# The forgetting bias of the attention logits as one bf16 product of three parts

## Chip, core and metric

One core of a Trainium2 chip runs the whole program in one launch. The metric is the device time of that core in microseconds (us), as the median of several runs; smaller is better.

## What is computed

The reference is one layer of an encoder: 16 learned tokens are put ahead of 512 frames of width 1024; a mixer made of forgetting attention and a state-space scan (S5) adds to the residual, then a product-key expert layer (PEER) adds to it, then a norm. All arrays are float32. What the change touches is the bias of the attention logits:

```python
log_f = jax.nn.log_sigmoid((f + b_forget).astype(jnp.float32))
cum = jnp.cumsum(log_f, axis=1)
s = jnp.einsum('bqhd,bkhd->bhqk', qb, kf)
s = s + cb[..., :, None] - cum_k[:, :, None, :]
s = jnp.where(mask, s, NEG_INF)
p = jax.nn.softmax(s, axis=-1)
```

The term of the query (`cb`) is constant along a softmax row and drops out, so the kernel adds only the negative running sum over the keys.

## The kernel before

The 512 frames are worked in two halves of 256 (hf = 0, 1), each of two tiles of 128 queries. For each half the program runs projections (queries, keys, values, the scan's input u), then a **mixer pass**, then branch products, the output product, a second norm and the query lists of the expert layer. The 512 gathered expert rows per partition (L635 on POOL, L1294 and L1297 on VectorE) are spread over what follows: 12 before the second pass, two with each of its steps, and so on by fixed counts, the rest in the last loop, which streams the expert tables through TensorE (L920, L929) from about 860 us to the end.

Each engine has its own instruction list, written out by hand, and they meet through semaphores; a table `order` at the top gives each product its pair of PSUM banks. A mixer pass has 16 steps. Step i handles one (tile j, head h) of the attention and one block i of 128 states of the scan, side by side:

- TensorE: `logits` of step i+1; a quarter of a gate product (`gate_part`, L681); the scan's output product `c_times_x` (L724, L725), which waits for POOL's `state`; another quarter; the transposes of the probabilities (L747, L749); a quarter; probabilities times values (L759, L761); a quarter; the scan's input products `b_times_u` (L715) for the step after.
- VectorE: the row maximum of the logits (L1356), then the scan's recurrence `recur` (L1182, L1324 to L1329), then the normalisation of the probabilities (L1360, L1361), in the second pass two expert rows (L1294).
- POOL: `state` (L579 to L586), in the second pass two gathers (L635).
- ScalarE: exponentials (L1004) and evacuations.

Tile j sees 16 + 128 (j+1) keys, so the four blocks of eight heads have 144, 272, 400 and 528 keys (blocks 0 and 1 in the first pass, 2 and 3 in the second). `logits` makes three kinds of products into one pair of banks: queries times keys (L737, 64 rows deep), the bias (L739), and the causal mask (L740, bf16, 128 columns). With 528 keys L737 and L739 are two products each of 264 columns. The bias is a product of a stationary operand that is one column of the identity, repeated 128 times (8 rows deep), and the 8 x 528 array `ncum`, the negative running sums of the eight heads. Both are float32; a float32 product stands in the profile as two MATMUL rows and two LDWEIGHTS rows, a bf16 product as one of each.

`ncum` is made once, on 8 partitions, before the first pass: VectorE adds the bias and forms a log-sigmoid with ScalarE (L1269 to L1275), clears an addend (L1276) and scans (L1277); the scan signals `ncum_ready`, for which TensorE waits before its first pass. Meanwhile POOL builds the table of rotations for the scan (L544 to L555, after L1080 gives sine and cosine) and signals `table_ready` behind L558, for which VectorE waits before its first pass. POOL's constants (identity, mask and others, L513 to L523) are made at the very start and signal `consts_ready`.

Of the kernel before, what the change touches and what calls it, by code (L numbers as in the profile page):

```python
# [15 lines left out]
ALU = mybir.AluOpType  # L16
# [3 lines left out]
BF16 = mybir.dt.bfloat16  # L20
# [3 lines left out]
P = 128  # L24
# [4 lines left out]
L = META + SEQ  # L29
TT = SEQ // P  # L30
HEADS = 8
# [41 lines left out]
O_ATT = O_VM + AW  # L73
# [9 lines left out]
O_NCUM = O_KEYS + HK * NKEY  # L83
# [29 lines left out]
def hybrid_program(nc, x, meta, g_mix, g_ffn, g_ffn_row, g_out, w_u, w_k, w_q, w_v, w_f, w_g, b_f, b_g, w_att, w_val,  # L113
# [53 lines left out]
    with ExitStack() as ctx:  # L167
        sb = lambda name, shape, dt=F32: ctx.enter_context(nc.sbuf_tensor(name, shape, dt))
        sem = lambda name: ctx.enter_context(nc.semaphore(name))
        gate_all = sb("gate_all", [P, G_WORDS])  # L170
# [14 lines left out]
        ident = sb("ident", [P, P])  # L185
        identb = sb("identb", [P, P], BF16)
        maskb = sb("maskb", [P, P], BF16)

        gathered = ring[:, 0:SLOTS, :]  # L190
# [25 lines left out]
        def shaped(v, shape):  # L216
            if len(shape) == 1:
                return v
            if len(shape) == 2:
                return v.rearrange("p (a b) -> p a b", a=shape[0])  # L220
            if len(shape) == 3:
                return v.rearrange("p (a b c) -> p a b c", a=shape[0], b=shape[1])
            return v.rearrange("p (a b c d) -> p a b c d", a=shape[0], b=shape[1], c=shape[2])

        def region(off, *shape):
            return shaped(gate_all[:, off:off + math.prod(shape)], shape)
# [8 lines left out]
        small, carry = region(O_SMALL, 34, NT), region(O_CARRY, 8, NT)  # L235
        gates, merged = region(O_GATES, 2 * DC, HALF), region(O_MERGED, DC, HALF)
        keysT = region(O_KEYS, HK, NKEY)
        ncum = gate_all[0:HEADS, O_NCUM:O_NCUM + L]
        ptmp = region(O_PTMP, SLOT)
        gg_sig, val_gated = region(O_GG, 2, HALF), [region(O_GG + 2 * HALF, HALF), region(O_PT, HALF)]  # L240
        fgate = region(O_ATT, 2, L)
        x_first, x_meta = region(O_GATES, TT, D), region(O_KEYS, D)
        gain = region(O_GATES, D)
        braw, bd = region(O_MERGED, 4, NT, GCH), region(O_MERGED + 4 * NT * GCH, 2, NT, 32)
# [68 lines left out]
        f_shifted, f_logged, ncum_ready = sem("f_shifted"), sem("f_logged"), sem("ncum_ready")  # L313
# [26 lines left out]
        def vacant(eng, name):  # L340
            if before[name]:
                eng.wait_ge(psum_drained[place[name][0]], before[name])
# [163 lines left out]
        def _(pool):  # L506
            steps = [0]

            def chain(ins):
                steps[0] += 1  # L510
                ins.then_inc(pool_step, 1)
                pool.wait_ge(pool_step, steps[0])
            chain(pool.memset(ident[:], 0.0))  # L513
            chain(pool.affine_select(out=ident[:], in_=ident[:], compare_op=ALU.not_equal, fill=1.0, base=0,
                                     pattern=[[-1, P]], channel_multiplier=1))
            chain(pool.tensor_copy(identb[:], ident[:]))
            chain(pool.memset(maskb[:], 0.0))

            chain(pool.affine_select(out=maskb[:], in_=maskb[:], compare_op=ALU.is_ge, fill=NEG, base=0,
# [11 lines left out]
            n, lvl = 1, 0  # L531
# [122 lines left out]
        def _(pe):  # L654
# [72 lines left out]
            def logits(j, h):  # L727
                n, at = META + (j + 1) * P, KEYS0[j]
                spans = [(0, n)] if at == 0 else [(0, BANK - at), (BANK - at, n)]
                name, hp, b = ("S", j, h), h // 2, 64 * (h % 2)  # L730
                vacant(pe, name)
                q = qT[j // 2][b:b + 64, hp, (j % 2) * P:(j % 2 + 1) * P]
                eh = ident[0:HEADS, h:h + 1].to_broadcast([HEADS, P])
                S = pair(name)

                for lo, hi in spans:
                    pe.matmul(S[:, at + lo:at + hi], q, kT[b:b + 64, hp, lo:hi], start=True, stop=False)  # L737
                for lo, hi in spans:
                    pe.matmul(S[:, at + lo:at + hi], eh, ncum[:, lo:hi], start=False, stop=(hi < n))  # L739
                pe.matmul(S[:, at + n - P:at + n], identb[:], maskb[:], start=False, stop=True)\  # L740
                  .then_inc(full_sem(name), 1)

# [95 lines left out]
            for dst, lo, hi in ((X0, 0, BANK - X0), (BANK, BANK - X0, L)):  # L838
                for c in range(DC):
                    mm = pe.matmul(pair(("f", 0))[0:HEADS, dst:dst + hi - lo], wf[:, c, :], hnT[:, c, lo:hi],  # L840
                                   start=(c == 0), stop=(c == DC - 1))
# [328 lines left out]
        def _(dve):  # L1170
            steps = [0]

            def step(ins):
                steps[0] += 1
                ins.then_inc(dve_step, 1)
                return steps[0]

            def chain(ins):
                dve.wait_ge(dve_step, step(ins))
# [35 lines left out]
            S = lambda k: small[:, k, :]  # L1215
# [43 lines left out]
            for g in range(2):  # L1259
                r = slice(64 * g, 64 * g + 64)  # L1260
# [5 lines left out]
            fx, fe = fgate[0:HEADS, 0, :], fgate[0:HEADS, 1, :]  # L1266
# [7 lines left out]
            chain(dve.scalar_tensor_tensor(out=fe, in0=fx, scalar=0.0, in1=fe, op0=ALU.min, op1=ALU.subtract))  # L1274
            chain(dve.tensor_scalar(fe, fe, -1.0, None, ALU.mult))  # L1275
            chain(dve.memset(fx, 0.0))  # L1276
            dve.tensor_tensor_scan(ncum, fe, fx, 0.0, ALU.add, ALU.add).then_inc(ncum_ready, 1)  # L1277

            emitted = [0]

# [212 lines left out]
            with dve.Fori(0, HALF // 16) as it:  # L1493
                for b in range(4):
# [6 lines left out]
                    for t in range(4):  # L1501
                        at = it * 16 + b * 4 + t
# [83 lines left out]
```

## Time and profile before

| | |
|---|---|
| Median of 3 runs | 1836.97 us (1836.08 to 1837.43) |
| The profiled execution | 1831.96 us |
| Its span in the trace | 1830.1 us |
| TensorE, VectorE, ScalarE, POOL busy | 1689.9, 1183.9, 305.4, 898.2 us |
| Granted TensorE clock, mean | 0.964 |
| Clock, 170 to 232 us (first pass, block 1) | 1.00 |
| Clock, 480 to 550 us (second pass, mostly block 2) | 0.93 |
| Clock, 550 to 600 us (second pass, block 3) | 1.00 |

How to read it: the span runs from the first to the last instruction of one execution; the execution's own time is a little longer. Busy times of engines overlap.
### The profile page before, as it was taken

What the parts mean: (1) busy time and instruction counts of PE and PEld (TensorE: products, weight loads), DVE (VectorE), ACT (ScalarE), POOL (GpSimd) and SP (SyncE); (2) the same over time, 40 slices, a digit from 0 to 9 for tenths busy, and PEclk for the clock granted to TensorE, in tenths of its full rate; (3) what the DMA queues carried; (4) which work ended last, traced back from release to release, by engine and by line L of the source; (5) the groups of instructions that cost most, each with busy time, mean ns of one, the idle gap of its engine ahead of it and who ended that gap; (6) DMA issues with size and microseconds to landing.
All of it is one profiled execution on the core that took longest, in us unless ns stands there. A gap on an engine that the chain in (4) does not pass through costs nothing.

```text
span 1830.1 us, 20496 instructions
## 1 busy us (share of the span) xinstructions
PE 1689.9 (92%) x6646; PEld 1148.5 (63%) x6646; DVE 1183.9 (65%) x2636; ACT 305.4 (17%) x718; POOL 898.2 (49%) x1125
## 2 busy tenths in 40 slices
PE   7989999997999689928799999999999999999996
PEld 6556675883566465817666666666666666666664
DVE  4156522697788354889866667667766666666666
ACT  3122231120222211118700000000100000000001
POOL 5955400386777442670045444455545455545442
PEclk9989999997999899959999999999999999999998
DMA  6312155547444683500089999999999999999997
GB/s 221 104 46 70 35 167 167 155 136 285 138 150 146 253 298 127 187 1 0 34 339 409 409 409 409 409 409 407 403 410 409 409 409 407 406 409 409 409 405 293
DMA packets 138092, 489.48 MB, mean 267 GB/s; under 512 B 16384, under 2 KB 16896, under 8 KB 137744
## 3 DMA queue, kind: packets, MB, share of 16 engines
q0 software_dynamic: 73728, 268.47, 37.7%
q1 hardware_dynamic: 64272, 219.85, 32.7%
q8 instruction: 50, 0.82, 0.2%
q14 instruction: 42, 0.34, 0.1%
HBM read 483.53 MB, written 4.72 MB: 267 GB/s over the span
## 4 chain that ended last, share of the span: by engine, by line
DMA 42%; PE 17%; POOL 16%; DVE 14%; issue 9%; ACT 1%; DVEq 0%; SPq 0%; POOLq 0%; ACTq 0%
DMA ring<-in_expert_v,chosen 23%; DMA ring<-in_expert_rows,chosen 17%; PE pair L669 8%; POOL ring L635 4%; DVE ring L1297 3%; DVE ring L1294 2%; POOL gate_all L584 2%; PE pair L942 2%; POOL temp L583 2%; PE pair L859 2%; PE pair L887 2%; DVE temp L1503 1%; POOL gate_all L580 1%; POOL gate_all L585 1%; PE pair L702 1%
## 5 line engine op out<-in xcount | busy, mean ns | idle before, releaser
L929 PE MATMUL pair<-temp,hnT 128*128 128x512 f32 x1024 | 463.4, 595 | 10.9 <-DVE hnT L1182 10.8
L920 PE MATMUL pair<-hnT,temp 128*128 128x256 f32 x2048 | 465.8, 381 | 3.8 <-DMA temp<-in_expert_u 3.8
L920 PEld LDWEIGHTS pair<-hnT,temp 128*128 128x128 f32 x2048 | 391.2, 191 | 111.7 <-issue 64.2
L635 POOL DMA_INDIRECT ring<-in_expert_rows,chosen x256 | 269.0, 1051 | 387.2 <-DVE ring L1294 350.7
L1297 DVE SCALAR_TENSOR_TENSOR ring<-ring,chosen 128x1024 f32<-128x1024 f32 x256 | 328.8, 1284 | 159.0 <-DMA ring<-in_expert_v,chosen 157.2
L1294 DVE SCALAR_TENSOR_TENSOR ring<-ring 128x1024 f32<-128x1024 f32 x256 | 327.5, 1290 | 143.5 <-DMA ring<-in_expert_rows,chosen 142.9
L635 POOL DMA_INDIRECT ring<-in_expert_v,chosen x256 | 261.2, 1020 | 264.4 <-DVE ring L1297 238.8
L929 PEld LDWEIGHTS pair<-temp,hnT 128*128 128x128 f32 x1024 | 193.4, 190 | 208.3 <-issue 201.3
L1156 ACT ACTIVATE hnT<-pair 128x256 f32<-128x256 f32 x128 | 49.0, 384 | 817.1 <-PE pair L920 817.1
L669 PE MATMUL pair<-hnT,gate_all 128*128 128x256 f32 x448 | 103.6, 387 | 1.4 <-issue 1.4
L669 PEld LDWEIGHTS pair<-hnT,gate_all 128*128 128x128 f32 x448 | 85.5, 195 | 12.8 <-issue 1.6
L942 PE MATMUL pair<-temp 128*128 128x128 f32 x512 | 72.6, 285 | 14.4 <-DVE temp L1503 14.3
L942 PEld LDWEIGHTS pair<-temp 128*128 128x128 f32 x512 | 62.4, 192 | 24.7 <-ACT temp L1127 24.0
L1356 DVE TENSOR_REDUCE st<-pair 128x1 f32<-128x144 f32 (+3 forms) x32 | 16.2, 507 | 88.0 <-PE pair L740 88.0
L681 PE MATMUL pair<-hnT,ring 128*128 128x256 f32 x256 | 72.3, 406 | 0.5 <-ACT gate_all L981 0.5
L1503 DVE TENSOR_SCALAR temp<-iota,chosen 128x128 f32<-128x128 f32 x256 | 70.3, 330 | 0.0
L579 POOL TENSOR_TENSOR gate_all<-temp,gate_all 128x256 f32<-128x256 f32 x32 | 23.2, 726 | 91.3 <-DVE temp L1329 91.3
L1182 DVE TENSOR_TENSOR hnT<-hnT,gate_all 128x256 f32<-128x256 f32 x128 | 54.2, 423 | 20.5 <-ACT hnT L1156 18.0
L669 PE MATMUL pair<-hnT,ring 128*128 128x272 f32 (+1 forms) x256 | 59.3, 392 | 1.5 <-DVE hnT L1182 1.5
L1182 DVE TENSOR_TENSOR gate_all<-pair,gate_all 128x256 f32<-128x256 f32 x32 | 13.6, 424 | 70.8 <-PE pair L669 52.2
L669 PEld LDWEIGHTS pair<-hnT,ring 128*128 128x128 f32 x256 | 49.3, 194 | 10.9 <-issue 2.4
L606 POOL TENSOR_TENSOR ring<-ring 128x32 f32<-128x32 f32 x8 | 2.2, 271 | 107.7 <-DVEq L1453 107.7
(264 smaller groups left out, 2002.2 us busy)
## 6 DMA issues: line engine op xcount, KB each, us to landing
temp<-in_expert_u SPq DMA_DIRECT2D x128, 512.0 KB, 6.8
temp<-in_expert_v SPq DMA_DIRECT2D x128, 512.0 KB, 6.8
gate_all<-in_w_query SPq DMA_DIRECT2D x24, 512.0 KB, 3.8
ring<-in_w_g SPq DMA_DIRECT2D x16, 512.0 KB, 3.5
ring<-in_w_u SPq DMA_DIRECT2D x8, 512.0 KB, 4.5
ring<-in_w_out SPq DMA_DIRECT2D x8, 512.0 KB, 4.9
temp<-in_w_query SPq DMA_DIRECT2D x8, 512.0 KB, 3.6
ring<-in_expert_rows,chosen POOLq DMA_INDIRECT x256, 10.3
```

The lines of the kernel that those rows point to most:

```text
L583: chain(pool.tensor_tensor(xs[0], pa, pb, ALU.subtract))
L635: pool.indirect_dma_start(out=gathered[:, g % SLOTS, :], out_offset=None, in_=(expert_rows, expert_v_rows)[part], in_offset=bass.IndirectO ...
L669: mm = pe.matmul(pair(name)[:, 0:width], w[:, c, :], rhs[:, c, lo:lo + width], start=(c == 0), stop=(c == kc - 1))
L681: mm = pe.matmul(pair(name)[:, 0:HALF], w[:, c, :], hnT[:, c, lo:lo + HALF], start=(c == 0), stop=(c == DC - 1))
L920: mm = pe.matmul(u_out[n % 2], u_in[:, n % 2, c * P:(c + 1) * P], hnT[:, c, FIRST[1]:L], start=(c == 0), stop=(c == DC - 1))
L929: mm = pe.matmul(pairs[i][:, b * 512:(b + 1) * 512], act[n % 2][:, i * P:(i + 1) * P], v_in[:, n % 2, b * 512:(b + 1) * 512], start=False, ...
L942: mm = pe.matmul(pairs[2 + s // 2][:, (s % 2) * 512 + t * P:(s % 2) * 512 + (t + 1) * P], oh2[s][:, t], oh1[:, s, t], start=True, stop=True)
L1156: ac.activation(act[n % 2], u_out[n % 2], ACT.Gelu).then_inc(gelu_done, 1)
L1182: return dve.tensor_tensor(out, a, b, ALU.mult)
L1294: dve.scalar_tensor_tensor(out=slot, in0=slot, scalar=1.0, in1=xrow, op0=ALU.mult, op1=ALU.mult, accum_out=wsel[:, at:at + 1]).then_inc(ro ...
L1297: dve.scalar_tensor_tensor(out=fin, in0=slot, scalar=wsel[:, at:at + 1], in1=fin, op0=ALU.mult, op1=ALU.add).then_inc(row_done, 1)
L1503: ins = dve.tensor_scalar(oh1[:, b, t], iota[:], first_key[:, bass.ds(at, 1)], gate_chosen[:, bass.ds(at, 1)], ALU.is_equal, ALU.mult)
```

## The change

`ncum` is cut into three bf16 parts, each the rounded rest of the ones before, which together give the float32 value. They stand on partitions 0 to 7, 32 to 39 and 64 to 71 of one bf16 array whose other rows are zero, and the stationary operand `one_head` has the head's column of an identity in each of the three places. So L739 becomes a single bf16 product 72 rows deep in place of a float32 product 8 rows deep, with the same columns. VectorE makes the parts behind the scan in six more operations; POOL makes `one_head` in three casts and clears the parts in one fill, among the first constants.

```diff
+        one_head = sb("one_head", [P, HEADS], BF16)
...
-        ncum = gate_all[0:HEADS, O_NCUM:O_NCUM + L]
+        fgate = region(O_ATT, 2, L)
+        ncum = gate_all[0:HEADS, O_ATT + 2 * L:O_ATT + 3 * L]
+        ncum_parts = region(O_NCUM, L // 2).bitcast(BF16)
+        second_part = fgate[0:HEADS, 0, 0:L // 2].bitcast(BF16)
...
             chain(pool.tensor_copy(identb[:], ident[:]))
+            for k in range(3):
+                r = slice(32 * k, 32 * k + 32)
+                chain(pool.tensor_copy(one_head[r, :], ident[r, 32 * k:32 * k + HEADS]))
+            chain(pool.memset(ncum_parts, 0.0))
...
-                eh = ident[0:HEADS, h:h + 1].to_broadcast([HEADS, P])
+                eh = one_head[0:64 + HEADS, h:h + 1].to_broadcast([64 + HEADS, P])
...
-                    pe.matmul(S[:, at + lo:at + hi], eh, ncum[:, lo:hi], start=False, stop=(hi < n))
+                    pe.matmul(S[:, at + lo:at + hi], eh, ncum_parts[0:64 + HEADS, lo:hi], start=False, stop=(hi < n))
...
-            dve.tensor_tensor_scan(ncum, fe, fx, 0.0, ALU.add, ALU.add).then_inc(ncum_ready, 1)
+            chain(dve.tensor_tensor_scan(ncum, fe, fx, 0.0, ALU.add, ALU.add))
+            chain(dve.tensor_copy(ncum_parts[0:HEADS, :], ncum))
+            chain(dve.tensor_tensor(fe, ncum, ncum_parts[0:HEADS, :], ALU.subtract))
+            chain(dve.tensor_copy(second_part, fe))
+            chain(dve.tensor_tensor(fe, fe, second_part, ALU.subtract))
+            dve.tensor_copy(ncum_parts[32:32 + HEADS, :], second_part)
+            dve.tensor_copy(ncum_parts[64:64 + HEADS, :], fe).then_inc(ncum_ready, 1)
```

No instruction changes its place; six are put in on VectorE between the scan and the first pass. Before, on VectorE, from the scan's last inputs to the first step of the first pass:

```order
L1275 TENSOR_SCALAR gate_all<-gate_all 8x528
L1276 MEMSET gate_all 8x528
L1277 SCALAR_TENSOR_TENSOR gate_all<-gate_all 8x528
L1356 TENSOR_REDUCE st<-pair 128x1
L1182 TENSOR_TENSOR temp<-pair,gate_all 128x272 x4
```

The same place after the change (the scan is L1284 there, the row maximum L1369, `recur`'s products L1189):

```order
L1282 TENSOR_SCALAR gate_all<-gate_all 8x528
L1283 MEMSET gate_all 8x528
L1284 SCALAR_TENSOR_TENSOR gate_all<-gate_all 8x528
L1285 CAST gate_all<-gate_all 8x528
L1286 TENSOR_TENSOR gate_all<-gate_all 8x528
L1287 CAST gate_all<-gate_all 8x528
L1288 TENSOR_TENSOR gate_all<-gate_all 8x528
L1289 COPY gate_all<-gate_all 8x528
L1290 CAST gate_all<-gate_all 8x528
L1369 TENSOR_REDUCE st<-pair 128x1
L1189 TENSOR_TENSOR temp<-pair,gate_all 128x272 x4
```

The six stand ahead of everything that VectorE does in the first pass, and the last of them gives the signal that the scan gave. On TensorE, at the first two steps, the list has the same rows; the bias product (L746 after the change) only reads another stationary tile:

```order
L722 MATMUL pair<-gate_all,chosen 128x272 x2
L744 MATMUL pair<-gate_all 128x144
L746 MATMUL pair<-gate_all,one_head 128x144
L747 MATMUL pair<-maskb,identb 128x128
L722 MATMUL pair<-gate_all,chosen 128x272 x2
```

## Rows read from the trace of the kernel before

**Rows 1.** Stretches in the second pass, block 2: us, length, busy us of each engine, clock, DMA

```profile
485.63:489.04 3.41, 3.41 (x9) 1.33 (x8) 3.27 (x9) 0.69 (x2) 2.88 (x4) 0.53 0.20 31
502.70:506.11 3.41, 3.41 (x12) 1.57 (x11) 3.41 (x6) 0.38 (x1) 3.33 (x3) 0.97 0.47 150
506.11:509.52 3.41, 3.41 (x9) 1.35 (x8) 3.27 (x8) 0.69 (x2) 2.88 (x4) 0.53 0.10 19
```

**Rows 2.** Order of time, block 0 (start us, length us, engine, line, operation, count)

```profile
121.86 0.51 PE L739 MATMUL pair<-gate_all,ident 8*128 8x144 f32 x2
...
122.30 0.23 PE L740 MATMUL pair<-maskb,identb 128*128 128x128 bf16 x1
...
130.39 0.72 POOL L586 TENSOR_TENSOR temp<-gate_all 128x256 f32<-128x256 f32 x1
...
131.35 0.62 PE L724 MATMUL pair<-temp,cd 128*32 128x256 f32 x2
```

**Rows 3.** Order of time, first pass, block 1

```profile
187.79 0.72 PE L739 MATMUL pair<-gate_all,ident 8*128 8x272 f32 x2
188.00 0.72 POOL L586 TENSOR_TENSOR temp<-gate_all 128x256 f32<-128x256 f32 x1
...
188.44 0.23 PE L740 MATMUL pair<-maskb,identb 128*128 128x128 bf16 x1
...
188.51 1.08 PE L681 MATMUL pair<-hnT,ring 128*128 128x256 f32 x4
...
189.52 0.62 PE L724 MATMUL pair<-temp,cd 128*32 128x256 f32 x2
```

**Rows 4.** Order of time, second pass, block 2

```profile
506.71 0.73 POOL L586 TENSOR_TENSOR temp<-gate_all 128x256 f32<-128x256 f32 x1
...
507.72 1.06 PE L724 MATMUL pair<-temp,cd 128*32 128x256 f32 x2
...
515.99 0.93 PE L739 MATMUL pair<-gate_all,ident 8*128 8x400 f32 x2
515.99 0.72 POOL L586 TENSOR_TENSOR temp<-gate_all 128x256 f32<-128x256 f32 x1
...
516.86 0.23 PE L740 MATMUL pair<-maskb,identb 128*128 128x128 bf16 x1
...
517.93 0.62 PE L724 MATMUL pair<-temp,cd 128*32 128x256 f32 x2
```

**Rows 5.** Order of time, second pass, block 3

```profile
567.99 1.15 PE L739 MATMUL pair<-gate_all,ident 8*128 8x264 f32 x4
...
569.08 0.23 PE L740 MATMUL pair<-maskb,identb 128*128 128x128 bf16 x1
...
569.15 0.72 POOL L586 TENSOR_TENSOR temp<-gate_all 128x256 f32<-128x256 f32 x1
...
570.16 0.62 PE L724 MATMUL pair<-temp,cd 128*32 128x256 f32 x2
```

**Rows 6.** Order of time, end of the second pass, where TensorE waits for POOL

```profile
610.34 0.72 POOL L586 TENSOR_TENSOR temp<-gate_all 128x256 f32<-128x256 f32 x1
...
611.21 0.59 PE L724 MATMUL pair<-temp,cd 128*32 128x256 f32 x2 [2.49 <-POOL temp L586]
```

**Rows 7.** Order of time on POOL, VectorE and TensorE, start and entry of the first pass

```profile
16.89 0.23 POOL L544 TENSOR_TENSOR gate_all<-gate_all 128x16 f32<-128x16 f32 x1 [12.67 <-ACT gate_all L1080]
...
78.88 2.17 DVE L1277 TENSOR_TENSOR_SCAN gate_all<-gate_all 8x528 f32<-8x528 f32 x1
...
80.02 3.19 POOL L546 TENSOR_TENSOR gate_all<-gate_all 128x1024 f32<-128x1024 f32 x1
...
93.84 1.15 PE L715 MATMUL pair<-gate_all,chosen 32*128 32x272 f32 x4 [1.31 <-ACT gate_all L981]
...
95.53 0.11 POOL L558 MEMSET gate_all<- 128x16 f32 x1
...
96.14 0.31 DVE L1356 TENSOR_REDUCE st<-pair 128x1 f32<-128x144 f32 x1 [15.09 <-PE pair L740]
```

More of the change, by code:

```diff
@@ L237, in hybrid_program @@
         keysT = region(O_KEYS, HK, NKEY)
-        ncum = gate_all[0:HEADS, O_NCUM:O_NCUM + L]
+        fgate = region(O_ATT, 2, L)
+        ncum = gate_all[0:HEADS, O_ATT + 2 * L:O_ATT + 3 * L]
+        ncum_parts = region(O_NCUM, L // 2).bitcast(BF16)
+        second_part = fgate[0:HEADS, 0, 0:L // 2].bitcast(BF16)
         ptmp = region(O_PTMP, SLOT)
         gg_sig, val_gated = region(O_GG, 2, HALF), [region(O_GG + 2 * HALF, HALF), region(O_PT, HALF)]
-        fgate = region(O_ATT, 2, L)
         x_first, x_meta = region(O_GATES, TT, D), region(O_KEYS, D)
```

## The prediction

> **What bounds the kernel now.** I read the page first. It says TensorE 92% busy and a chain that ends in DMA, but both are averages over stages. The edited product (L739) runs only in the two mixer passes (the first begins at 93.84 us [rows 7], the second ends just behind 611.21 [rows 6]), so those decide. The busy time of stretches shows TensorE busy 3.41 of 3.41 us in both passes' middle, so every nanosecond of L739 is TensorE's own time there, with the clock at its lower level in one stretch of six out of the second pass's first block [rows 1]. The order of time then shows what else turns in the same circle. Step i of a mixer is one (tile, head): TensorE makes logits(i+1), part 0 of a gate product, then c_times_x(i) (L724), which needs POOL's state(i). VectorE starts its recurrence for a head only behind the row maximum of that head's logits, and POOL follows it. So there are two circles: TensorE's work of one step, and a circle over two steps, L724(i-1), logits(i+1), VectorE, POOL, L724(i+1). How close the second is to the first is read as the gap between the end of POOL's L586 and the start of L724, less the 0.15 us that a hand-over takes where TensorE truly waited (610.34+0.72 to 611.21) [rows 6]:
> - block 0 (144 keys): 131.35 - (130.39+0.72) - 0.15 = 0.09 us [rows 2]
> - block 1 (272 keys): 189.52 - 188.72 - 0.15 = 0.65 us [rows 3]
> - block 2 (400 keys): 507.72 - 507.44 - 0.15 = 0.13 us where the clock is low, 517.93 - 516.71 - 0.15 = 1.07 us in the next step [rows 4]
> - block 3 (528 keys, two products): 570.16 - 569.87 - 0.15 = 0.14 us [rows 5]
>
> TensorE binds everywhere, but in blocks 0, 2 and 3 POOL is only a tenth of a microsecond behind.
>
> **The product (L739).** From its start to the start of the mask product it takes 122.30-121.86 = 0.44, 188.44-187.79 = 0.65, 516.86-515.99 = 0.87 and 569.08-567.99 = 1.09 us in blocks 0 to 3 [rows 2 to 5]. The nearest row for a bf16 product is the mask product, 128 columns: 0.07 us until the next one starts [rows 3]. In proportion to columns the new one takes 0.08, 0.15, 0.22 and 0.29 us; adding 0.1 us per product for a weight load that may show gives 0.18, 0.25, 0.32 and 0.49. That it sums over 72 rows where it was 8 is covered by this price, as the mask product sums over 128. I take savings x of 0.36, 0.50, 0.65 and 0.75 us; the far ends are 0.26, 0.40, 0.55 and 0.59.
>
> TensorE's step gets shorter by x. The circle over two steps holds one logits product of its two, so it shortens by x while two of TensorE's steps shorten by 2x. A step therefore gains the smaller of x and (gap + x)/2:
> - block 0: (0.09+0.36)/2 = 0.22 us, 5 steps: 1.1
> - block 1: x = 0.50 (the other is 0.57), 8 steps: 4.0
> - block 2, if the clock falls as now: (0.13+0.65)/2 = 0.39 us, 5 steps: 2.0
> - block 3: (0.14+0.75)/2 = 0.44 us, 8 steps: 3.5
>
> Three of a pass's heads stand outside this: the first two run before the circle turns, where VectorE and POOL are late anyway (nothing), and the third gains its full x, 0.36 and 0.65 us. Sum of the product: 1.1+4.0+2.0+3.5+1.0 = 11.6 us, of 24.4 us (8 times the four durations) that L739 holds. The rest becomes TensorE's wait for POOL at L724.
>
> **The six new VectorE operations** (8x528, behind the scan L1277). The scan ends at 81.05 [rows 7]. TensorE needs them when it enters the mixer, with L715 at 93.84, so 12.8 us are free [rows 7]. Beside POOL's table building the scan over these 528 elements took 2.17 us [rows 7]. Six like it, each behind its forerunner by 0.04 us, are 13.3 us; the lower bound is nothing. I expect some 11 us, near the upper end, as only the last two meet short POOL operations. Hidden, barely; at the upper end the mixer starts 0.5 us late.
>
> What isn't hidden is POOL. Its table must be complete (L558, ends 95.64) before VectorE enters the mixer, and VectorE's first reduction stands at 96.14 [rows 7], so there is under half a microsecond of room. L546 (80.02) took 3.19 us, of which 1.03 passed before the scan had ended [rows 7]: a VectorE operation beside it can cost a POOL operation up to 1 us. The six new ones cost it between nothing and 6 us; they are shorter than the scan and some meet the gaps, so I take a third of a microsecond each, 2 us, which leaves VectorE's start 1.5 us later (with 0 and 3 kept for the range, since most of the table is done by then). About half comes back, as less TensorE work then falls into the low-clock stretch at the start of the pass: I count 0.7 us net.
>
> The Trainium skill (SBUF, State Buffer on-chip working memory, "Who interferes with whom") calls the pair of ports that VectorE and GpSimd share an exclusive lock, held for a whole instruction and taken by copies, casts and two-input operations. By that rule all six collide, POOL loses their whole length and the start comes 3 us later, which would make the sum 0.8 us worse than I have it; the scan's 2.17 us beside L546's 3.19 agrees with the rule [rows 7].
>
> **The POOL additions at the start** (three casts of 32x8, one fill) are 1 to 1.5 us ahead of the table, but POOL then idles 12.67 us until the sine and cosine are there [rows 7], and the constants are needed by TensorE only after the first norm: nothing. **Everything behind** (branch products, queries, lists, expert loop) starts from the end of a mixer and moves with it; its weight loads are gated by the same progress, and the number of expert rows gathered early is fixed by the program.
>
> **Sum**: -11.6 + 0.7 = -10.9 us. The profiled execution (1831.96 us, span 1830.1) goes to about 1821.1. It was 5 us under the median of the runs, 1836.97; against that median I forecast **1826.0 us**. A change under 0.2% (3.7 us) can't be told from none. With the far ends of x (gains 0.17, 0.40, 0.34, 0.36 a step, 0.8 for the third heads: 9.4) and 3 us of late start it is -6.4, 1830.6.
>
> **Rivals.**
> - *The falls of the clock go away.* The stretch at 506.11 ran at 0.53, right behind one (502.70) in which TensorE did the products with few rows (L715, L737, L739); the fall at 485.63 is the same thing two steps earlier [rows 1]. One costs 0.47 x 3.41 = 1.6 us. With L739 shorter these stretches hold more full products. Without falls a step of block 2 takes (20.48 - 1.07 - 0.65)/2 = 9.4 us against 10.24 now, 0.85 gained instead of 0.39, 2.3 us over five steps, and 1.6 for the fall ahead of them: -14.8, 1822.2 us. For it: block 2 is the only one with regular falls and has long few-row products. Against: TensorE will now wait up to 0.6 us a step right behind them.
> - *The start is dearer*: the six operations end too late, the mixer starts 3 us later and the low clock stays one stretch more (1.6 us): -11.6+3+1.6 = -7.0, 1830.0 us.
> - *No change that can be measured*: the 72-row product with a broadcast one-column stationary runs no faster than the float32 one, or VectorE or POOL slow down as they crowd together: between 0 and -3 us, 1835.5. For it: POOL is already within 0.1 us in three blocks. Against: block 1 has room.
> - *Slower: the clock falls every second head of both passes.* Place: the stretches around logits, in which TensorE now both does less and waits. Price 1.6 us a fall; the 28 heads of the steady part allow 14 falls where there are 4 now, 10 x 1.6 = 16 us: -10.9+16 = +5, 1842 us. It decides from nine additional falls. Against it: blocks 1 and 3 ran at full clock throughout (the small table above). The Trainium skill (TensorE: Matmul & The Clock Gate, "What's actually happening") says the default state is throttled and activity releases it, and that rule is this rival's ground.
>
> **Chances.** Forecast 0.50, no falls 0.20, dear start 0.12, no change 0.13, slower 0.05. The likeliest case gives the time; the range 1821.0 to 1832.0 takes in the first three. Faster by over 0.2%: the first three and a sliver of the fourth, 0.84; within 0.2%: 0.12; slower 0.04.
>
> **What would show it.** Right: L739's successor at about 0.1 us to 0.3 us per head; a step of block 1 shorter by half a microsecond; L724 in block 3 now waiting for POOL's L586; VectorE's row maximum waiting less for TensorE; the six operations at 1 to 2.4 us each, and VectorE's first row maximum near 97.5 us. Wrong: the same step times with longer idle time of TensorE, or a lower granted clock in blocks 1 and 3.

## Result and profile after

| | before | after |
|---|---|---|
| Median of the runs beside each other | 1837.20 us (1836.08 to 1841.31, 4 runs) | 1817.33 us (1814.51 to 1817.97, 4 runs) |
| Profiled execution, its span | 1831.96, 1830.1 us | 1817.97, 1816.1 us |
| TensorE, VectorE, POOL busy | 1689.9, 1183.9, 898.2 us | 1660.8, 1194.9, 903.6 us |
| Clock, 480 to 550 us | 0.93 | 1.00 |

After to before is 0.9897 [0.9879, 0.9915]: 18.9 us saved (15.6 to 22.2), where the prediction had 10.9 and a range down to 16. The direction was right; the measured time, 1817.33, lies below the range's low end, 1821.0.

I cut both traces at VectorE's row maximum, which runs once a head: 16 in the first pass (blocks 0, 1), 16 in the second (blocks 2, 3). The stages of the two profiled executions, in us:

| | before | after | difference |
|---|---|---|---|
| start to first row maximum | 96.1 | 96.5 | +0.4 |
| first pass, 1st to 16th row maximum | 127.5 | 121.2 | -6.3 |
| 16th to 17th (rest of the head, branches, second pass's lead-in) | 220.6 | 222.3 | +1.7 |
| second pass, 17th to 32nd | 156.1 | 146.8 | -9.3 |
| everything behind | 1229.8 | 1229.4 | -0.4 |

The five make the -14.0 us between the spans. The two passes give 15.6 us, the second half as much again as the first. The 1.7 us lost between them is no effect of the change that can be told: in the twelve traces of this document that stage takes 220.6 to 222.8 us.

The product itself, in the order of time of TensorE after the change (start us, length us, engine, line, operation, count, in brackets the wait ahead of it); blocks 0, 1, 2 and 3:

```profile
121.03 0.24 PE L746 MATMUL pair<-gate_all,one_head 72*128 72x144 bf16 x1
121.11 0.22 PE L747 MATMUL pair<-maskb,identb 128*128 128x128 bf16 x1
...
184.49 0.29 PE L746 MATMUL pair<-gate_all,one_head 72*128 72x272 bf16 x1
184.62 0.22 PE L747 MATMUL pair<-maskb,identb 128*128 128x128 bf16 x1
...
517.75 0.40 PE L746 MATMUL pair<-gate_all,one_head 72*128 72x264 bf16 x2
517.99 0.22 PE L747 MATMUL pair<-maskb,identb 128*128 128x128 bf16 x1
...
519.49 0.59 PE L731 MATMUL pair<-temp,cd 128*32 128x256 f32 x2 [0.36 <-POOL temp L593]
...
566.49 0.40 PE L746 MATMUL pair<-gate_all,one_head 72*128 72x264 bf16 x2
566.72 0.22 PE L747 MATMUL pair<-maskb,identb 128*128 128x128 bf16 x1
...
568.43 0.59 PE L731 MATMUL pair<-temp,cd 128*32 128x256 f32 x2 [0.57 <-POOL temp L593]
```

From the product's start to the mask product's it is 0.08, 0.13 and 0.23 us in blocks 0, 1 and 3 (0.44, 0.65 and 1.09 before [rows 2, 3, 5]); L731, which was L724, now waits for POOL in blocks 2 and 3. (517.75 is block 3's first head, with two products; block 2's is shown further down.)

The step time of block 1 and of block 3, from VectorE's row maximum to the next one, after the change:

```profile
184.88 0.44 DVE L1369 TENSOR_REDUCE st<-pair 128x1 f32<-128x272 f32 x1 [3.12 <-PE pair L747]
193.07 0.44 DVE L1369 TENSOR_REDUCE st<-pair 128x1 f32<-128x272 f32 x1 [3.13 <-PE pair L747]
...
557.44 0.71 DVE L1369 TENSOR_REDUCE st<-pair 128x1 f32<-128x528 f32 x1 [1.26 <-PE pair L747]
566.98 0.71 DVE L1369 TENSOR_REDUCE st<-pair 128x1 f32<-128x528 f32 x1 [0.77 <-PE pair L747]
577.03 0.71 DVE L1369 TENSOR_REDUCE st<-pair 128x1 f32<-128x528 f32 x1 [0.43 <-PE pair L747]
```

and the same of before, block 3:

```profile
559.05 0.71 DVE L1356 TENSOR_REDUCE st<-pair 128x1 f32<-128x528 f32 x1 [1.50 <-PE pair L740]
569.35 0.71 DVE L1356 TENSOR_REDUCE st<-pair 128x1 f32<-128x528 f32 x1 [1.52 <-PE pair L740]
```

Block 1 takes 8.19 us a step (8.73 before). Block 3 takes 9.54 and 10.05 in turn, 9.8 on average, against 10.29; that two steps alternate fits the circle over two steps. VectorE's wait for TensorE fell, in block 3, from 1.5 us to 0.4 to 1.3.

In block 2 the fall of the clock is gone. Busy time of each engine by stretches, with the granted clock and the DMA share behind, after the change:

```profile
475.00:530.00 55.00, 51.36 (x238) 31.78 (x236) 49.10 (x87) 13.91 (x41) 48.57 (x48) 1.00 0.55 170
```

and before:

```profile
475.00:530.00 55.00, 55.00 (x220) 31.72 (x220) 45.30 (x83) 12.56 (x37) 42.88 (x43) 0.91 0.49 152
```

TensorE was busy all 55 us at a mean clock of 0.91 and is now busy 51.4 us at full clock: the rest, 3.6 us, is its wait for POOL.

The start, VectorE and POOL after the change:

```profile
78.74 2.17 DVE L1284 TENSOR_TENSOR_SCAN gate_all<-gate_all 8x528 f32<-8x528 f32 x1
80.94 2.40 DVE L1285 CAST gate_all<-gate_all 8x528 bf16<-8x528 f32 x1
...
87.73 2.74 DVE L1288 TENSOR_TENSOR gate_all<-gate_all 8x528 f32<-8x528 f32 x1
90.51 0.29 DVE L1289 COPY gate_all<-gate_all 8x528 bf16<-8x528 bf16 x1
90.81 0.42 DVE L1290 CAST gate_all<-gate_all 8x528 bf16<-8x528 f32 x1
96.51 0.31 DVE L1369 TENSOR_REDUCE st<-pair 128x1 f32<-128x144 f32 x1 [5.28 <-POOL gate_all L565]
...
96.36 0.11 POOL L565 MEMSET gate_all<- 128x16 f32 x1
```

The six operations end at 91.23, 10.3 us behind the scan, and VectorE then waits 5.28 us for POOL. What the six cost POOL is read from the scan's end: its table is complete 15.45 us behind it (96.36 less 80.91), before 14.48 (95.53 less 81.05 [rows 7]), so 0.97 us more; in before_again and after_again it is 14.48 and 15.46. The first row maximum comes 0.37 us later by the clock of the traces, which is no more than they scatter (96.14 and 97.00 in the two of the kernel before); behind the scan's end it stands at 15.09 and 15.17 us before and at 15.60 in both traces of the change.

### The profile page after: what moved, and what is told of

Read it like the earlier page. It is cut to its first block, busy times and chain, and to the rows that moved or that the text cites. A ratio compares the mean times of both kernels' runs of the same rounds, so it can differ in the third digit from the quotient of the medians.

```text
span 1816.1 us, 20426 instructions
## 1 busy us (share of the span) xinstructions
PE 1660.8 (91%) x6606; PEld 1136.0 (63%) x6606; DVE 1194.9 (66%) x2642; ACT 305.3 (17%) x718; POOL 903.6 (50%) x1129
## 4 chain that ended last, share of the span: by engine, by line
DMA 43%; POOL 20%; DVE 14%; PE 13%; issue 9%; ACT 1%; DVEq 0%; SPq 0%; POOLq 0%; ACTq 0%
DMA ring<-in_expert_v,chosen 24%; DMA ring<-in_expert_rows,chosen 17%; PE pair L676 5%; POOL ring L642 4%; DVE ring L1310 3%; DVE ring L1307 2%; POOL gate_all L591 2%; POOL temp L590 2%; PE pair L949 2%; PE pair L866 2%; PE pair L894 2%; DVE temp L1516 1%; POOL gate_all L587 1%; POOL gate_all L592 1%; POOL temp L593 1%
## 5 line engine op out<-in xcount | busy, mean ns | idle before, releaser
L1189 DVE TENSOR_TENSOR hnT<-hnT,gate_all 128x256 f32<-128x256 f32 x128 | 54.2, 424 | 24.2 <-ACT hnT L1163 21.7
L1189 DVE TENSOR_TENSOR gate_all<-pair,gate_all 128x256 f32<-128x256 f32 x32 | 13.6, 424 | 72.3 <-PE pair L676 54.9
L1369 DVE TENSOR_REDUCE st<-pair 128x1 f32<-128x144 f32 (+3 forms) x32 | 16.2, 507 | 62.5 <-PE pair L747 57.2
L722 PE MATMUL pair<-gate_all,chosen 32*128 32x272 f32 (+1 forms) x128 | 38.8, 423 | 18.9 <-DVE temp L1189 16.3
## 6 DMA issues: line engine op xcount, KB each, us to landing
ring<-in_expert_rows,chosen POOLq DMA_INDIRECT x256, 10.3
```

Source lines behind the costliest of these rows:

```text
L722: pe.matmul(pair(name)[:, 0:WIDTH[hf]], bT[q:q + 32, a, i // 4, :], uT[hf][q:q + 32, i // 4, :], start=True, stop=True).then_inc(full_sem( ...
L1189: return dve.tensor_tensor(out, a, b, ALU.mult)
```

## Experiments

The theory: the saving is TensorE's time at the bias product, handed on until POOL limits, and in block 2 the falls of the clock have gone with it. Its rivals: the rest comes from somewhere else in the program, or the falls come and go by chance. There are ten runs, the two kernels again and eight others; ratios are to the kernel before on the same chip. The columns of the passes are from each profiled execution (us); in brackets stands the pass without its first two steps. Falls are separate low-clock stretches between the second pass's lead-in and its last row maximum. The last column is the granted clock as a mean over all executions of the run; over 60 executions of the kernel before it is 0.9640.

| | median (runs) | ratio | first pass | second pass | falls | clock |
|---|---|---|---|---|---|---|
| kernel before (first profile) |  |  | 127.5 (109.03) | 156.1 (135.19) | 4 |  |
| change (first profile) | 1817.33 (4) | 0.9897 [0.9879, 0.9915] | 121.2 (103.89) | 146.8 (125.15) | 0 | 0.967 |
| before_again | 1836.40 (12) | 1.0007 [0.9993, 1.0021] | 127.5 (109.03) | 154.9 (132.71) | 2 | 0.9632 |
| parts_only | 1835.97 (12) | 1.0003 [0.9989, 1.0017] | 127.4 (109.03) | 158.0 (136.13) | 3 | 0.9631 |
| dense_rows | 1828.42 (12) | 0.9965 [0.9952, 0.9978] | 126.3 (107.75) | 152.0 (129.71) | 0 | 0.9670 |
| first_pass_bf16 | 1831.03 (12) | 0.9980 [0.9965, 0.9995] | 121.2 (103.89) | 159.3 (138.43) | 5 | 0.9623 |
| second_pass_bf16 | 1822.51 (6) | 0.9936 [0.9913, 0.9959] | 127.2 (109.03) | 146.7 (125.15) | 0 | 0.9670 |
| after_again | 1816.17 (5) | 0.9904 [0.9881, 0.9928] | 121.5 (103.92) | 145.5 (125.14) | 0 | 0.9676 |
| no_bias | 1816.53 (6) | 0.9897 [0.9877, 0.9918] | 120.2 (102.97) | 144.3 (123.84) | 0 | 0.9660 |
| recur_first | 1826.15 (9) | 0.9952 [0.9936, 0.9969] | 127.5 (110.70) | 146.5 (127.52) | 0 | 0.9667 |
| one_part | 1819.28 (6) | 0.9911 [0.9895, 0.9927] | 123.5 (104.79) | 150.6 (130.29) | 3 | 0.9675 |
| full_rows_bf16 | 1816.77 (5) | 0.9893 [0.9877, 0.9909] | 122.4 (103.89) | 146.0 (125.12) | 0 | 0.9678 |

The brackets tell the product's effect cleanly. In the first pass they are 109.03 us wherever the bias product is the 8-row float32 one and VectorE's order the same, and 103.89 to 103.92 with 72 or 128 bf16 rows. The first two steps vary with the place of the low-clock stretch at the start: in the kernel before it ends 13.8 us behind the first row maximum and the two steps take 18.5 us, in the change 12.2 and 17.3, in full_rows_bf16 14.7 and 18.5. In the second pass 72 or 128 bf16 rows give 125.1 us every time, and the kernels with falls give 130.3 to 138.4.

One more low-clock stretch stands 10 to 12 us behind the last row maximum in seven of the twelve traces (the two of the kernel before, parts_only, first_pass_bf16, dense_rows, after_again, no_bias), so it goes with neither the rows nor the type of the product.

### Both kernels again

The two kernels unchanged, on another chip.

> The kernel before once more, for its own spread. If the profiled execution shown (1831.96 us) was only a quick draw of the same kernel, this one comes out near 1836 to 1837 us, with more or longer stretches at the lower clock in the passes or other stages than the first trace had; a ratio of 1.000 within 0.002. If the two loads of the program differ for another reason, the clock list is the same and the time is lost in one stage, which the trace then names.

> The change once more. Theory: ratio 0.990 within 0.002 (some 18 to 20 us), first pass 4 to 6 us shorter from its first to its last row maximum, second pass 9 us shorter, of which about 3 to 4 us because the three regular falls of the clock in block 2 are gone. Rival: the falls come and go by chance; then this trace has some in block 2 again and the time rises by 2 to 5 us.

Before came out at itself, the change at 0.9904: the gain repeats. Against what I expected, the kernel before was slower here (1837.00 us in the profiled execution) with two falls fewer: its second pass is 1.2 us shorter, and what it loses stands behind the passes (1234.3 us against 1229.8). The two kernels differ in how steady they are: 29 runs of the kernel before on this chip spread from 1828.39 to 1839.25 us, 5 of the change from 1815.70 to 1818.46.

### Parts made, product left in float32

The edit against the kernel before; `ncum` stays where it was, the parts get a place of their own.

```diff
             chain(pool.tensor_copy(identb[:], ident[:]))
+            for k in range(3):
...
+            chain(pool.memset(ncum_parts, 0.0))
...
-            dve.tensor_tensor_scan(ncum, fe, fx, 0.0, ALU.add, ALU.add).then_inc(ncum_ready, 1)
+            chain(dve.tensor_tensor_scan(ncum, fe, fx, 0.0, ALU.add, ALU.add))
+            chain(dve.tensor_copy(ncum_parts[0:HEADS, :], ncum))
...
+            dve.tensor_copy(ncum_parts[64:64 + HEADS, :], fe).then_inc(ncum_ready, 1)
```

> The three parts and the one-head tile are made as in the change, but the logits take the float32 product as before. Theory: the six operations are hidden before the first pass and only POOL's table comes later, so the first row maximum is 0.4 to 1 us later and the whole 0 to 1.5 us slower (ratio 1.000 to 1.001). Rival: the gain of the change comes partly from the moved start (another place of the clock's low stretch); then this one is faster than before by 2 us or more.

1.0003 [0.9989, 1.0017]. Making the parts costs nothing that can be told; the gain lies in the product.

### Either pass alone

Blocks of the first pass are `j` 0 and 1, of the second 2 and 3. The change, with the old product kept in one pass (here the second; for second_pass_bf16 the condition is `j < 2`). The parts lie in an array of their own, so that both forms are there:

```diff
+                eh = one_head[0:64 + HEADS, h:h + 1].to_broadcast([64 + HEADS, P])
+                bias = ncum_parts[0:64 + HEADS, :]
+                if j >= 2:
+                    eh, bias = ident[0:HEADS, h:h + 1].to_broadcast([HEADS, P]), ncum
```

> The change, but blocks 2 and 3 (the second pass) keep the float32 bias product; both forms of the running sums are kept. Theory of the paths: the first pass from first to last row maximum 6.3 us shorter than before (127.5 to 121.2), the second as before with its falls of the clock (155 to 158 us); the whole 5 to 7 us faster, ratio 0.9965 to 0.997. Rival (the gain is mostly the absence of falls in the second pass): a whole within 3 us of before.

> The other half: blocks 0 and 1 keep the float32 product. Theory: the first pass stays at 127.5 us, the second goes from 155 to 158 down to 145.5 to 147 us with no fall of the clock in blocks 2 and 3; the whole 9 to 12 us faster, ratio 0.9935 to 0.995. With the other half the two should add up to the change.

The first half alone saves 0.2% (3.7 us), the second 0.64% (11.7 us). Each has in its own pass the time that the full change has there (103.89 and 125.15 us without the first two steps). The first half lost part of its 6.3 us again: its second pass took 159.3 us, with five falls and this clock:

```profile
475.00:530.00 55.00, 55.00 (x215) 31.85 (x214) 46.39 (x81) 12.48 (x37) 42.92 (x43) 0.88 0.50 155
```

So the falls go with the old product in the second pass, and their number varies: two to five in the four traces that have it there. The granted clock over all executions says the same: 0.9623 on average over the 12 of the first half, 0.9670 over the 6 of the second.

### The old float32 product, 128 rows deep

This changes nothing about the float32 product but its depth: the other 120 rows are zero.

```diff
+        ncum_all = region(O_NCUM, L)
...
+            chain(pool.memset(ncum_all, 0.0))
...
-                eh = ident[0:HEADS, h:h + 1].to_broadcast([HEADS, P])
+                eh = ident[:, h:h + 1].to_broadcast([P, P])
...
-                    pe.matmul(S[:, at + lo:at + hi], eh, ncum[:, lo:hi], start=False, stop=(hi < n))
+                    pe.matmul(S[:, at + lo:at + hi], eh, ncum_all[:, lo:hi], start=False, stop=(hi < n))
```

> Before, with the float32 bias product made 128 rows deep instead of 8 (the other rows are zero): the same columns, passes and duration on TensorE, one more fill on POOL at the start. If the falls of the clock in block 2 came from the few rows of L739, they go: three falls of 1.6 us less, and the time falls by 3 to 6 us (ratio 0.997 to 0.998), with a granted clock of 1.00 in block 2. If rows play no part, the falls stay, at 20.5 us from each other, and the ratio is 1.000.

0.9965, that is 6.4 us, without bf16 and without parts. Order of time on TensorE, block 1:

```profile
187.18 0.72 PE L741 MATMUL pair<-gate_all,ident 128*128 128x272 f32 x2
187.74 0.22 PE L742 MATMUL pair<-maskb,identb 128*128 128x128 bf16 x1
```

Start to start it is 0.56 us where 8 rows took 0.65 [rows 3], and the step of block 1 is 8.62 us instead of 8.73. In block 2 no fall is left, and steps take 9.33 and 9.96 us instead of 9.43 and 11.07. Steps of the old product that no fall meets take 9.43 and 9.96 in before_again. So of the 0.75 us a step that the full change gained in block 2, 0.55 is the clock's. The trace has one fall, 11.8 us behind the last row maximum. Over all 12 executions the granted clock is 0.9670 on average; before_again, on the same chip, has 0.9632.

### bf16 product 8 rows deep

Of the change, the first part alone: the bias is rounded to bf16, and the other two parts with five of the VectorE operations are left out.

```diff
-                eh = one_head[0:64 + HEADS, h:h + 1].to_broadcast([64 + HEADS, P])
+                eh = one_head[0:HEADS, h:h + 1].to_broadcast([HEADS, P])
...
-                    pe.matmul(S[:, at + lo:at + hi], eh, ncum_parts[0:64 + HEADS, lo:hi], start=False, stop=(hi < n))
+                    pe.matmul(S[:, at + lo:at + hi], eh, ncum_parts[0:HEADS, lo:hi], start=False, stop=(hi < n))
```

> The change with the first bf16 part alone: a product 8 rows deep, and five of the six operations left out (the bias is rounded to bf16). If the columns of the product make its time, L746 still takes 0.08, 0.13 and 0.23 us, or up to 0.1 us more per product, if the few rows delay what follows, as they did for the float32 product (0.65 against 0.56 us); the first row maximum comes 0.3 to 0.5 us earlier. If the falls of the clock in block 2 hang on how long the few-row products last in all, they stay away, since L746 is short; if the 72 rows were needed against them, they return, and with them the spread of the runs (10 us in before, 3 us in the change). I expect no falls, and a ratio of 0.990.

I had expected no falls. The profiled execution has three in block 2, where steps alternate between 8.84 and 11.55 us. But it is the slowest of six: two took 1824.19 and 1823.74 us, at a granted clock of 0.966 and 0.965, four took 1818.40 to 1819.33 at 0.967 to 0.970. Three falls at 1.7 us each are 5.1 us, which is the distance between the two groups (an estimate; only one execution has a trace). So with this product falls came in one trace and most likely in two executions of six, while the old float32 product has them in all four of its traces.

Order of time on TensorE at the first steady step of block 2, 8 rows:

```profile
470.77 0.34 PE L746 MATMUL pair<-gate_all,one_head 8*128 8x400 bf16 x1
471.04 0.23 PE L747 MATMUL pair<-maskb,identb 128*128 128x128 bf16 x1
471.11 1.08 PE L688 MATMUL pair<-hnT,temp 128*128 128x256 f32 x4
473.26 1.03 PE L731 MATMUL pair<-temp,cd 128*32 128x256 f32 x2 [1.07 <-POOL temp L593]
```

and the stretches of that kernel there:

```profile
470.10:473.50 3.40, 2.33 (x9) 1.06 (x9) 3.02 (x8) 0.69 (x2) 3.18 (x4) 0.95 0.40 139
473.50:476.90 3.40, 3.40 (x10) 1.79 (x9) 3.29 (x7) 0.38 (x1) 3.08 (x4) 0.55 0.53 153
```

The full change, 72 rows:

```profile
469.88 0.34 PE L746 MATMUL pair<-gate_all,one_head 72*128 72x400 bf16 x1
470.06 0.22 PE L747 MATMUL pair<-maskb,identb 128*128 128x128 bf16 x1
470.12 1.08 PE L688 MATMUL pair<-hnT,temp 128*128 128x256 f32 x4
472.38 0.59 PE L731 MATMUL pair<-temp,cd 128*32 128x256 f32 x2 [1.19 <-POOL temp L593]
```

with

```profile
470.10:473.50 3.40, 2.21 (x11) 1.16 (x10) 3.11 (x10) 0.74 (x3) 3.18 (x4) 1.00 0.24 98
```

Both wait for POOL right behind the few-row products, the 72-row kernel even longer, and it is busy less (2.21 us against 2.33). Yet it keeps the full clock, and the 8-row kernel runs the next stretch at 0.55. This pair alone doesn't settle it, because the step lies elsewhere relative to the clock's last rise: L746 starts 14.7 us behind it with 8 rows and 13.0 with 72. after_again, where it is 14.4 us behind, is nearer:

```profile
469.26 0.34 PE L746 MATMUL pair<-gate_all,one_head 72*128 72x400 bf16 x1
471.75 0.59 PE L731 MATMUL pair<-temp,cd 128*32 128x256 f32 x2 [1.18 <-POOL temp L593]
...
469.40:472.80 3.40, 2.22 (x11) 1.13 (x9) 3.10 (x10) 0.69 (x2) 3.17 (x4) 1.00 0.26 106
```

It has no fall either. But parts_only, with the old 8-row product 14.2 us behind the rise, has none at this step too; its first comes later in the block. So with 8 rows falls come, and whether one comes at a given step varies. That the rows and not the type of the product make the difference is shown for float32 (dense_rows); for bf16 it rests on this one trace. The price is firm: the 8-row product costs more by itself, 0.27 us until its successor starts where the 72-row one takes 0.18, as in float32.

### bf16 product 128 rows deep

```diff
-            for k in range(3):
+            for k in range(4):
...
-                eh = one_head[0:64 + HEADS, h:h + 1].to_broadcast([64 + HEADS, P])
+                eh = one_head[:, h:h + 1].to_broadcast([P, P])
...
-                    pe.matmul(S[:, at + lo:at + hi], eh, ncum_parts[0:64 + HEADS, lo:hi], start=False, stop=(hi < n))
+                    pe.matmul(S[:, at + lo:at + hi], eh, ncum_parts[:, lo:hi], start=False, stop=(hi < n))
```

> The change with a fourth, zero group, so that the bias product is 128 rows deep. If nothing hangs on rows any more, L746 and the steps stay as in the change (7.7, 8.2, 9.5, 9.8 us), ratio 0.990. If 128 rows still free what follows, as they did for float32, each step gets up to 0.09 us shorter and the whole up to 2 us.

0.9893 [0.9877, 0.9909], the change's own ratio, no falls, and the same steps. 72 rows are enough here.

### No bias product

This kernel leaves the forgetting term out of the logits.

```diff
-                    pe.matmul(S[:, at + lo:at + hi], q, kT[b:b + 64, hp, lo:hi], start=True, stop=False)
-                for lo, hi in spans:
-                    pe.matmul(S[:, at + lo:at + hi], eh, ncum_parts[0:64 + HEADS, lo:hi], start=False, stop=(hi < n))
+                    pe.matmul(S[:, at + lo:at + hi], q, kT[b:b + 64, hp, lo:hi], start=True, stop=(hi < n))
```

> The change with the bias product left out altogether (logits without the forgetting term); the parts are still made. TensorE gains a further 0.08, 0.13, 0.17 and 0.23 us a step in blocks 0 to 3. If POOL's circle binds as the waits at L731 say, blocks 0, 2 and 3 gain only half of that, block 1 all of it: 2.5 us against the change, a ratio of 0.989 to before. If TensorE still binds everywhere, 4.5 us against the change.

Block 1 takes 8.08 us a step, 0.11 under the change, and the two passes together 264.5 us against 267.9 in the change and 267.0 in after_again. But the whole is at 1816.53 us no faster, where I had expected 2.5 us less. In the profiled execution the part behind the passes took the gain back (1232.2 us against 1229.4 and 1228.1), and this begins at the last head of the second pass. Order of time on TensorE:

```profile
594.01 1.03 PE L731 MATMUL pair<-temp,cd 128*32 128x256 f32 x2 [1.97 <-POOL temp L593]
594.83 1.06 PE L732 MATMUL pair<-temp,cd 128*32 128x256 f32 x2
```

and the stretches:

```profile
590.40:593.80 3.40, 1.16 (x5) 0.68 (x4) 1.41 (x2) 0.38 (x1) 3.24 (x4) 0.96 0.34 77
593.80:597.20 3.40, 3.19 (x7) 1.71 (x8) 0.54 (x1) 0.38 (x1) 2.64 (x4) 0.50 0.42 110
597.20:600.60 3.40, 3.40 (x12) 2.31 (x11) 0.00 (x0) 0.74 (x2) 1.20 (x2) 0.54 0.91 312
```

TensorE was busy 1.16 of 3.40 us, waiting for POOL, and then ran 6.8 us at the lower level. It isn't the leaving out of the product that brings this: both traces of the change have the same wait at the same head. In the first the clock stays at full speed:

```profile
597.70 0.59 PE L731 MATMUL pair<-temp,cd 128*32 128x256 f32 x2 [2.04 <-POOL temp L593]
...
594.20:597.60 3.40, 1.13 (x4) 0.68 (x4) 1.29 (x2) 0.28 (x1) 3.19 (x4) 1.00 0.24 77
```

In after_again, with 2.06 us of wait, it falls for 3.4 us. So a wait of some 2 us at the same head was followed by no fall, one of 3.4 us or one of 6.8 us, and what the fall took from this execution (half of 6.8 us, 3.4) isn't shown to be a price of the faster product. The record allows only this: what remains of the bias product is worth 1.3 us in the second pass's last 13 steps and 0.9 in the first's, and nothing of it can be told in the whole.

### The recurrence ahead of the row maximum

If POOL now limits, VectorE should give it its input sooner.

```diff
+                    recur(hf, i)
                     filled(dve, name)
...
-                    recur(hf, i)
                     drained(dve, name)
```

> The change, and VectorE runs the recurrence of a step ahead of the row maximum, so that POOL's circle no longer holds the logits. If that circle binds blocks 0, 2 and 3 now, TensorE's wait at L731 goes and the steps fall to TensorE's own pace: 7.6, 8.2, 8.8 and 9.45 us, 7 to 8 us less than the change, a ratio of 0.986 to before. Rival: VectorE then waits for ScalarE's exponential in every step (about 1 us, with nothing to do) and becomes the bound with some 9.8 us in block 3; then the gain is 0 to 3 us, or the passes get longer.

1826.15 us, 8.8 above the change, where I had expected 7 to 8 below. In block 3 TensorE no longer waits for POOL; the wait is at the exponential, as the rival had it. Waits in a stretch of block 3 (engine, line, what it waited for, us in total, times, longest), this kernel:

```profile
DVE st L1373 <- ACT gate_all L1011: 4.3, 5, 0.9
PE pair L766 <- ACT gate_all L1024: 3.9, 6, 1.3
```

and the change:

```profile
PE pair L731 <- POOL temp L593: 1.7, 4, 0.6
```

The row maximum comes later, with it ScalarE's exponential, and VectorE stands 0.86 us a step for its sum. In the first pass this costs 6.3 us, the first row maximum comes 4.1 us later, and the second pass gains nothing (146.5 us, the change 146.8). The row maximum's place ahead of the recurrence is right here. No kernel here is faster than the change by more than the runs scatter.

## Why the prediction fell short

**Right.** The reading that TensorE binds and that POOL takes over at once in blocks 0, 2 and 3. The product's price: savings of 0.36, 0.52 and 0.86 us for blocks 0, 1 and 3, where I had 0.36, 0.50 and 0.75 (block 2, 0.87 [rows 4] less the 0.18 above, gives 0.69 for 0.65). Of the 0.1 us per product that I had added for a weight load nothing shows: 0.08, 0.13, 0.18 and 0.23 us is not even the share of columns, 0.08, 0.15, 0.22 and 0.29. The steps: 0.24 us gained in block 0 (0.22), 0.54 in block 1 (0.50), 0.5 in block 3 (0.44). The six operations took 10.3 us for "some 11", hidden, and making the parts costs nothing (parts_only). TensorE waits for POOL in block 3 as said. "The product is no faster", "a dear start" and "slower" did not happen; block 1 kept its full clock.

**Partly luck: the first pass.** It gave 6.3 us for 5.5 of the sum. Its last 13 steps gave 5.1. The other 1.2 came in the first two steps, which I had put at nothing, because the low-clock stretch there ended earlier against the work; in full_rows_bf16 they give nothing.

**The step that failed** is "block 2, if the clock falls as now: 0.39 us", and with it the 0.65 us of the third head. The rival *the falls of the clock go away* happened. Block 2's step was 10.24 us, averaged over one that a fall met and one that none met; it is 9.5, a gain of 0.75 a step where I had 0.39 and the rival 0.85. The third step of the second pass, where the first fall stood, got 2.34 us shorter (0.65 in the sum), the five behind it 3.22 (2.0), and the ninth, where the fourth fall stood, 1.73 (0.44). The whole pass gave 9.3 us where my sum had 6.15. The rival's sum was -14.8 us, and the profiled executions differ by -14.0.

I had the reason in hand, that each fall stands right behind the stretch with the few-row products [rows 1], and gave the rival 0.20 because TensorE would now wait behind them. The wait came, up to 1.2 us, and the clock stayed. The 8-row float32 product in the second pass: falls in four traces of four. 72 or 128 rows there, in float32 or bf16: none in six traces of six. The 8-row bf16 product: three falls in its one trace, and probably none in four of its six executions. My rival's own reason, "with L739 shorter", is not needed: dense_rows keeps its length nearly whole and has no fall. Whether a shorter product also makes falls rarer, as one_part's quick executions suggest, is open.

**Mis-sized: the start.** I took 1.5 us late, 0.7 on balance against me; it was 0.37. The six operations cost POOL 0.97 us, not 2. The long side was VectorE's: 2.0 to 2.7 us for each of the first four, beside POOL's operations of 1024 columns, 0.29 and 0.42 for the last two, beside short ones; the same cast took 2.40 us in the one place (L1285) and 0.42 in the other (L1290). The Trainium skill (SBUF — State Buffer, "Who interferes with whom") says that whichever of the two engines issues first has the shared pair of ports for its whole instruction and the other waits. I had let POOL lose every time, which that page doesn't say; the trace agrees with it in that it was mostly VectorE that lost.

**The base.** The measured 1817.33 us lies 8.7 us under my 1826.0. The profiled executions differ by 14.0 us where I had 10.9: 3.2 of the second pass, 0.9 of the first, 0.3 of the start and 0.5 at the end, less 1.8 in between. The other 5.6 us are the base, the larger part. The profiled execution of before was 5.0 us under its median; that of after, 1817.97, the slowest of its four. I carried a gain worked out on one execution over to the median as if the gap of 5 us would stay; even the rival's sum gave 1822.2 by that.

Why the gap went is shown in part. Executions of the kernel before vary by some 11 us on one chip, of the change by under 4, and with the time goes the granted clock: the ten of 60 under 1832 us have 0.966 on average, the thirteen over 1837 us 0.962. 0.004 of 1835 us is 7 us of the 9 between the groups (an estimate). That it isn't the second pass alone is seen in before_again: 1.2 us shorter there, 4.5 us longer behind it (1234.3 and 1229.8). Behind the second pass the six traces with a bf16 product throughout it have 1227.2 to 1229.6 us, and the six others, no_bias among them, 1229.8 to 1234.3. The time at the lower level in that part, without its last stretch at the very end, is 61.4 to 68.3 us in the first six and 71.7 to 75.1 in the others, 6.8 us less on average; half of it is 3.4, and so much less the part takes on average. Why the clock falls less often there, in code that is the same, stays open. The halves, too, add to 15.4 us where the whole gives 18.9, with intervals that allow it.

## What to carry to other kernels

Of a product on an engine that binds, read its rows as well as its columns: an 8-row product cost some 0.09 us more than a deep one, and the float32 one brought low-clock stretches behind it, so filling it up with zero rows alone was worth 0.35% here. When a profile shows falls behind such a place, price the case without them as a main case, and test it with the same product made deep. Look at the granted clock of every execution, not of the profiled one alone: it told here that one_part's trace was one of its two slow executions. And when one execution is the base of the sum, look at how far it stands from its median: if the change takes away something that varies, the gap can go too.

## What the hardware showed unexpectedly

- **Depth costs time when small.** A float32 product of 272 columns took 0.65 us with 8 rows [rows 3] and 0.56 with 128, start to start; the bf16 product of 400 columns 0.27 with 8 rows and 0.18 with 72.
- **The granted clock didn't follow TensorE's busy time.** Before, it fell to 0.53 behind a stretch that was busy 3.41 of 3.41 us [rows 1]; with 72 rows it stayed at 1.00 with 2.21 of 3.40 busy, and at the last head with 1.13 of 3.40. It did fall, with no bias product at all, behind 1.16 of 3.40, and in after_again behind the same wait. Deep products in place of the 8-row one took the falls out of the second pass's steps and raised the mean clock from 0.963 to 0.967; what the chip itself counts isn't seen in any trace, and no run moved the same work in time alone.
- **Falls come in a rhythm.** With the 8-row bf16 product, steps of 8.84 and 11.55 us alternate through block 2, one fall per two steps, and the four falls of the kernel before stand two steps from each other. With the 72-row product and no first fall the same heads take 9.35 to 9.6 us each. That one fall sets up the next is argued from this regular distance, not tested.
- **The work itself repeats to some 0.03 us in 100.** Behind its first two steps the first pass took 109.03 us in four traces with the old product in it, and 103.89 to 103.92 in four with 72 or 128 bf16 rows, on several chips. So a step time may be compared between single traces to a few hundredths, and the time of a whole execution may not.
